# Half slabs, another order of the first tiles, turns in the second router, and token lists multiplied on TensorE, in a two-layer diffusion backbone

## The reference, cut to what matters

```python
mod = (silu_c @ ada_w[l] + ada_b[l])[:, None, :]
sh1, sc1, g1, sh2, sc2, g2 = jnp.split(mod, 6, axis=-1)
hx = modulate(rms_norm(x, norm_mix_w[l]), sh1, sc1)     # h * (1 + scale) + shift
mx = even_mixer(hx, hc, w_in[li], ...) if even else pool_mixer(hx, ...)
x = x + g1 * mx
x = x + g2 * moe_ffn(modulate(rms_norm(x, norm_ffn_w[l]), sh2, sc2), router_w, router_b, ...)

def moe_ffn(h, router_w, router_b, w_gate, w_up, w_down):
    combine = moe_route(flat, router_w, router_b)       # sigmoid scores, top 2 inside one group of 4
    for e in range(N_EXPERTS):
        hid = jax.nn.silu(flat @ w_gate[e]) * (flat @ w_up[e])
        out = out + combine[:, e:e + 1] * (hid @ w_down[e])
```

## Time and profile before

| | |
|---|---|
| median of 3 runs | 1142.43 us (1141.96 to 1145.59) |
| profiled execution | 1138.41 us, span 1136.4 us |
| TensorE busy, share of span | 1007.8 us, 89% |
| VectorE busy | 937.8 us, 83% |
| ScalarE busy | 627.1 us, 55% |
| GpSimd busy | 141.7 us, 12% |
| mean granted TensorE clock | 0.961 of full |

### The profile page before, as it was taken

How to read it: one execution, slowest core, us unless ns; L and a number is a source line. 1 busy time by engine, 2 the same in 40 slices (tenths; PEclk the granted TensorE clock), 3 DMA queues, 4 the chain that set the end, 5 groups by cost and what they waited for, 6 DMA issues and landing times. The chain is left out here.

```text
span 1136.4 us, 14202 instructions
## 1 busy us (share of the span) xinstructions
PE 1007.8 (89%) x4910; PEld 804.5 (71%) x4910; DVE 937.8 (83%) x1037; ACT 627.1 (55%) x770; POOL 141.7 (12%) x176
## 2 busy tenths in 40 slices
PE   5888999998898996899999999928799999999980
PEld 1467777786666774788888888827578888888870
DVE  4578997895697865799999999856689999999975
ACT  1535322323476234677777777533467777777841
POOL 0100210000010002510000000041440000000006
PEclk9899999998899998999999999969899999999995
DMA  9726878844200645899999999967399999999946
GB/s 370 270 75 222 282 253 289 289 167 153 89 1 1 224 192 184 278 401 413 413 415 414 414 413 414 347 241 287 114 331 411 415 413 414 414 414 414 413 200 241
DMA packets 148822, 332.46 MB, mean 293 GB/s; under 512 B 16956, under 2 KB 18948, under 8 KB 148648
## 3 DMA queue, kind: packets, MB, share of 16 engines
q1 hardware_dynamic: 125768, 277.99, 64.3%
q10 hardware_dynamic: 15520, 28.68, 7.1%
q0 software_dynamic: 7488, 25.19, 5.9%
HBM read 308.72 MB, written 23.15 MB: 292 GB/s over the span
## 5 line engine op out<-in xcount | busy, mean ns | idle before, releaser
L1984 DVE TENSOR_TENSOR w_lo<-ring,w_hi 128x2048 fp32r<-128x2048 f32 x192 | 432.8, 2287 | 25.5 <-ACT w_hi L1820 22.9
L1820 ACT CAST w_hi<-ring 128x2048 fp32r<-128x2048 f32 x192 | 364.4, 1914 | 144.9 <-DMA ring<-in_moe_w_up 52.3
L2095 PE MATMUL bank<-w_hi,xT_hi 128*128 128x512 f32 x512 | 203.4, 397 | 8.1 <-DVE xT_lo L1991 5.2
L2095 PE MATMUL bank<-w_hi,xT_lo 128*128 128x512 f32 x512 | 199.9, 390 | 0.0
L2095 PE MATMUL bank<-w_lo,xT_hi 128*128 128x512 f32 x512 | 199.4, 390 | 0.0
L1478 PE MATMUL bank<-ring_last_parts,arena_parts 128*128 128x512 f32 (+1 forms) x320 | 117.2, 397 | 5.6 <-DVE ring_parts L1070 3.1
L2095 PEld LDWEIGHTS bank<-w_hi,xT_hi 128*128 128x128 f32 x512 | 96.2, 188 | 29.8 <-DVE xT_lo L1991 6.9
L2095 PEld LDWEIGHTS bank<-w_hi,xT_lo 128*128 128x128 f32 x512 | 96.1, 188 | 20.9
L2095 PEld LDWEIGHTS bank<-w_lo,xT_hi 128*128 128x128 f32 x512 | 96.2, 188 | 19.0
L1478 PE MATMUL bank<-ring_parts,arena_parts 128*128 128x512 f32 (+1 forms) x256 | 100.3, 392 | 0.0
L1131 DVE SCALAR_TENSOR_TENSOR gate_b<-ring,silu_c,gate_b 128x512 f32<-128x512 f32 x126 | 95.5, 758 | 4.5
(11 more groups left out here) (270 smaller groups left out, 1505.7 us busy)
## 6 DMA issues: line engine op xcount, KB each, us to landing
ring<-in_moe_w_gate SPq DMA_DIRECT2D x64, 1024.0 KB
ring<-in_moe_w_down SPq DMA_DIRECT2D x64, 1024.0 KB, 11.8
ring<-in_moe_w_up SPq DMA_DIRECT2D x64, 1024.0 KB, 13.4
ring<-in_ada_w SPq DMA_DIRECT2D x19, 2048.0 KB, 9.4
y_scratch<-shared ACTq DMA_DIRECT2D x30, 512.0 KB, 6.8
ring<-in_w_in ACTq DMA_DIRECT2D x21, 512.0 KB, 4.4
shared<-in_ada_w SPq DMA_DIRECT2D x3, 2048.0 KB, 15.4
x_res<-in_x SPq DMA_DIRECT2D x8, 512.0 KB, 11.9
```

The lines of the kernel that those rows point to most:

```text
L1820: nc.scalar.copy(w_hi[:, buf(u, p), :], half(raw(e, p))).then_inc(s_hi, 3 if isinstance(e, int) and (e, p) == (-1, 3) else 1)
L1984: V.tensor_tensor(w_lo[:, buf(u, p), :], half(raw(e, p)), w_hi[:, buf(u, p), :].bitcast(F32), ALU.subtract).then_inc(s_lo, 3 if isinstance ...
L2095: last = pe.matmul(bank[:, b, :], xs[:, kk, :], ws[:, k, :], start=(kk == 0 and i == 0), stop=(kk == KD - 1 and i == 2))
```

## The change

Four parts. **Loads and sums:** the four slabs are loaded in halves, in the order `PRE_ORDER`, all of them ahead of the tokens; seven constant loads go from ScalarE's queue to SyncE's, behind x5, and the zeroing of the lists goes away. VectorE sums slab 3 and then the first half of slab 2; TensorE adds its own matmuls of slab 2's second half to the pick of that sum. **First tiles:** other orders on ScalarE, VectorE and TensorE; the spot (0, 3) stands just ahead of (1, 3), and from quarter 2 on ScalarE casts w_hi(n + 1) ahead of the load of quarter n + 2. **Router of layer 1:** square(3) ahead of copy_T(1), and transposes(t) ahead of logits(t − 1). **Lists:** the places of the two chosen experts of a token become half-precision one-hots `slot_of`; eight small matmuls with `listed` (token number where the expert is chosen) make all 16 lists in one bank. Expert 0 keeps its own direct list. The fetches take their rows from `lists` with no cast. The path for over 128 tokens is made anew on the same principle.

```diff
+        PRE_ORDER = ((3, 0), (0, 0), (3, 1), (0, 1), (1, 0), (1, 1), (2, 0), (2, 1))
+        spots.remove((0, NT - 1))
+        spots.insert(spots.index((1, NT - 1)), (0, NT - 1))
...
+                for j, hf in PRE_ORDER:
+                    k = slice(hf * KD // 2, (hf + 1) * KD // 2)
+                    sp.dma_start(pre_slab(j)[:, k], slab(ada_w[0], j * HALF)[:, k]).then_inc(m_pl[j][hf], 16)
                 load_rows_of(0)
                 load_rows_of(1)
-                sp.dma_start(pre_slab(2), slab(ada_w[0], 2 * HALF)).then_inc(m_pl[2], 16)
...
                     if t == 0:
+                        if 2 <= n + 1 < NQ:
+                            w_hi(n + 1)
                         if 3 <= n + 2 < NQ:
                             act.wait_ge(m_pu, used(n - 1))
                             load_w(act, n + 2)
-                        if 2 <= n + 1 < NQ:
-                            w_hi(n + 1)
...
                 rows_of_slab(0, 0)
+                dve.wait_ge(m_pre, 2)
+                sum_of_pre(2, 0, KD // 2)
+                rows_of_slab(1, 3)
+                rows_of_slab(2, 1)
                 xhat_of(0)
                 xhat_of(1)
-                rows_of_slab(1, 1)
-                w_lo(0)
-                rows_of_slab(2, 3)
                 rows_of_slab(3, 2)
+                xhat_of(2)
...
                 h_rest(0)
+                w_lo(0)
+                h_low(0)
                 h_rest(1)
-                xhat_of(2)
-                h_low(0)
                 xhat_of(3)
+                h_low(1)
                 h_rest(2)
-                h_low(1)
+                w_lo(1)
+                h_low(2)
                 h_rest(3)
-                h_low(2)
                 h_low(3)
-                w_lo(1)
...
+                rows_of_pre(0, 0).then_inc(m_pre, 1)
+                rows_of_pre(1, 0, KD // 2)
+                pick_pre(3, 1, True).then_inc(m_pre, 1)
+                rows_of_pre(1, KD // 2).then_inc(m_pre, 1)
+                rows_of_pre(2, KD // 2, stop=False)
+                pick_pre(2, 2, False).then_inc(m_pre, 1)
                 transpose_x(0)
...
                     fetch(0, idx[:])
                     nc.gpsimd.memset(mark[:], 0.0).then_inc(s_first_rows, 1)
+                    pool.wait_ge(s_lists, 1)
+                    for m in range(1, NE):
+                        u = m % 2
+                        if m >= 2:
                             pool.wait_ge(s_gt, m - 1)
                             pool.wait_ge(s_xg[u], 16 * (m // 2))
+                        fetch(u, lists[:, m:m + 1])
...
+                    for c in range(2):
+                        ins = V.tensor_tensor(slot_of[:, c], places.unsqueeze(1).to_broadcast([P, NT, P]),
+                                              cols(place[:, c, :], P), ALU.is_equal)
+                    ins.then_inc(s_slots, 1)
...
                     low(-1, 0, 0)
+                    dve.wait_ge(s_in_lists, 1)
+                    V.tensor_copy(lists[:], bank[:, LIST_BANK, 0:NE]).then_inc(s_lists, 1)
+                    low(-1, 0, 1)
+                    rows_low(0, 0, None)
+                    low(-1, 0, 2)
+                    low(-1, 0, 3)
                     rows_of_tokens()
-                    rows_low(0, 0, None)
-                    for p in range(1, 4):
-                        low(-1, 0, p)
                     weights_of_tokens()
...
-                    keep_busy(10)
+                    keep_busy(6)
                     rows_T(0, 16)
...
-                for t in range(NT):
+                for t in range(NT - 1):
                     act.wait_ge(p_xr, t + 1)
                     front1.square(act, t)
-                    if t >= 1:
-                        front1.copy_T(act, t - 1)
-                front1.copy_T(act, NT - 1)
+                front1.copy_T(act, 0)
+                act.wait_ge(p_xr, NT)
+                front1.square(act, NT - 1)
+                for t in range(1, NT):
+                    front1.copy_T(act, t)
```

More of the change, by code:

```diff
@@ L574, in build_program @@
             transposes_after.setdefault(projected(u) - 1 + 4, []).append(r)
-        m_ld = {n: sem(f"m_ld_{n}") for n in ("ident", "smallA", "smallB", "rope", "row", "gap", "zero")}
+        m_ld = {n: sem(f"m_ld_{n}") for n in ("ident", "smallA", "smallB", "rope", "row", "gap")}
         m_x = [sem(f"m_x{t}") for t in range(NK)]
@@ L824, in _ @@
                 h_first(0)
+                h_high(0)
                 h_first(1)
-                h_high(0)
+                h_high(1)
                 h_first(2)
-                h_high(1)
+                h_high(2)
+                w_hi(1)
                 h_first(3)
-                h_high(2)
                 h_high(3)
-                w_hi(1)
                 squares_of(4)
@@ new lines, in _ @@
+                    for c in range(2):
+                        ins = V.tensor_tensor(r_tmp[:, c], pick[:, c], pos, ALU.mult)
+                    link(ins)
+                    link(V.tensor_reduce(place[:], r_tmp[:], AX.X, ALU.add))
+                    dve.wait_ge(s_first, 1)
+                    V.tensor_copy(idx[:], bank[:, FIRST_BANK, 0:1]).then_inc(s_first_idx, 1)
+                    for c in range(2):
+                        ins = V.tensor_tensor(slot_of[:, c], places.unsqueeze(1).to_broadcast([P, NT, P]),
+                                              cols(place[:, c, :], P), ALU.is_equal)
@@ L1951, in rows_of_tokens @@
+                    ins.then_inc(s_slots, 1)
                     def rows_of_tokens():
-                        for c in range(2):
-                            ins = V.tensor_tensor(r_tmp[:, c], pick[:, c], pos, ALU.mult)
-                        link(ins)
-                        link(V.tensor_reduce(place[:], r_tmp[:], AX.X, ALU.add))
                         V.scalar_tensor_tensor(row_tmp[:, 0], e_sel[:], float(P), place[:], ALU.mult, ALU.add)
@@ L2257, in _ @@
                         pe.transpose(bank[:, 5, 0:P], ident[:], ident[:]).then_inc(v_d, 1)
+                        for b in range(MORE):
+                            pe.wait_ge(v_slot, 2 * b + 2)
+                            if b >= 1:
+                                pe.wait_ge(v_lists, b)
+                            for c in range(2):
+                                for t in range(NT):
+                                    last = pe.matmul(bank[:, LIST_BANK, 0:NE], slot_of[:, c, t, :], listed[:, c, t, :],
+                                                     start=(c == 0 and t == 0), stop=(c == 1 and t == NT - 1))
+                            last.then_inc(v_in, 1)
+                        pe.wait_ge(v_lists, MORE)
                         for e, b, n in blocks(pe):
```

211 lines of the change are left out of this document (98 added, 113 removed).

## The result

The changed kernel takes 1132.33 us, the median of 7 runs (1129.51 to 1136.84), against 1141.96 for the kernel before in the same comparison: a ratio of 0.9924, 95% interval 0.9898 to 0.9950. Timed twice more beside other kernels it gave 0.9941 (0.9920 to 0.9962) and 0.9939 (0.9913 to 0.9965). So it is faster by 0.6 to 0.8%, 6 to 9 us. I had forecast 1140.7, with a range from 1135.5. The direction was right and the size was wrong by about 5 to 7 us in differences (1.7 forecast, 6.3 to 8.6 measured).

The account below looks back on a forecast made before the run. The prediction took TensorE to bound the experts, so that only its waits elsewhere could pay; the front's +3.2, layer 1's router's −2.4 and the lists' −2.5 summed to −1.7 us, a median of 1140.7, range 1135.5 to 1145.0.

Parts of the forecast that it names:

- A: Front of layer 0: an early start lost again and a likely clock fall, +3.2 us, ends −5.5 and +11.
- the base: Front of layer 0: quarter 4's first matmul moves from 79.20 to 80.3, +1.0 us at full clock.
- the 2.2 us for the clock: Front, behind x4: about 4.5 us of TensorE work at clock 0.50 adds 2.2 us, quarter 4 at 82.5.
- the head start: Front: first projection matmul 5.5 us sooner, at 39.1; quarter 3's load then waits for spot (0,3) until 61.3.
- C: Layer 1's router: earlier square(3) and transposes start the sigmoid at 797.7 instead of 800.13, −2.4 us, between −1 and −3.
- M: Lists, both expert layers: without scatters the first experts' waits for weights go, −2.5 us, between −3.8 and +1.
- The gather of expert 1: Start of the experts: issued later, behind the lists' copy, +0.3 us per layer (0 to 0.9), 0.6 in all.
- the upper end of 0.9 per layer: Expert 1's fetch: VectorE shutting GpSimd out of the common port would cost 0.9 us per layer, making the lists' term −1.3.
- the filler's cut to six: Ahead of rows_T(0): keep_busy(10) to (6) costs 0.8 to 1.9 us per layer if the clock falls, otherwise nothing.
- rival (1): Front keeps full clock or part of its early start: +1.0 to −0.5 there, total −3.9 to −5.4, about 1138; chance 0.25.

Follow-up runs that it names:

- A and C: The changed kernel with the lists made by scatters again, as in the kernel before: 1136.15 us, ratio 0.9994 to before.
- C alone: The kernel before with only the two new orders in layer 1's router: 1134.66 us, ratio 0.9958.
- C and M: The kernel before with the new router orders and the lists multiplied on TensorE, front as before: 1130.86 us, ratio 0.9941 to before.
- A alone: The kernel before with only the new front (loads, sums, first tiles), zeroing of the lists kept on SyncE's queue: 1138.54 us, ratio 0.9999.
- A and M: The changed kernel with layer 1's router in its old order: 1134.60 us, ratio 0.9973 to before.
- scatters kept: The changed kernel with eight scatters per layer kept as idle work into a list nobody reads: 1135.23 us, ratio 0.9958 to before.
- the two edits: On the changed kernel, separately: spot (0,3) in its old place, 1127.63 us (again 1125.59); tile 4's work ahead of the quarter 0 buffer wait, 1127.43 us.
- before again: The kernel before, unchanged, timed and profiled again: 1138.75 us, ratio 1.0000.
- tile 4 early: The changed kernel with tile 4's work ahead of quarter 0's buffer wait (ScalarE) and w_lo(3) (VectorE), tile 5's second half too: 1127.43 us, ratio 0.9898 to before.

## Why the prediction was wrong

**A, the front (+3.2 forecast, 0 measured): two terms failed. The base, "Carried on, the first matmul of quarter 4 [...] falls on 80.3: +1.0 with the clock at full speed", was 2 us too late, and the 2.2 us for the clock were added whole, though waits behind it take over part of them.** In the first trace the steps up to there seem to hold: TensorE's start 8.98 (9.2 forecast), the first normalized tile 34.03 (35.1), the first projection matmul 38.08 (39.1), x4's transposes 55.47 (57.4) behind a pause of 3.63 (4.4), quarter 3's load at 60.97 (61.3), x5 at 67.27 (68.0) behind 3.55 (4.2). But the last two were forecast for full clock, and in this trace the clock fell in both places. The Trainium skill ("TensorE: Matmul & The Clock Gate", section "HAM oscillation — how this bites in real kernels") says the same of such waits, and the windows (0.57, and 0.50 from 68 to 72) agree; in the kernel's second trace, with a pause of 3.63 ahead of x5 too, they show 1.00.

That second trace is the test of the base. There the load is issued at 59.86, x5's transposes stand at 66.23 and quarter 4 at 78.24; with A and C, the other trace of this front without such a fall, quarter 4 stands at 78.40. That is −1.0 and −0.8 against 79.20, not +1.0, though in both the clock had been at 0.50 for a while from 47 on, ahead of x4. In the five traces of this front with falls quarter 4 begins 0.9 to 2.4 us later than 78.24 (79.16 to 80.65, never 82.5), and quarter 6 0.9 to 1.7 later. In the kernel before, TensorE waits 1.22 us for VectorE at 79.20 and 1.49 at 94.03, and VectorE's dense stretch begins at 71.72 in it and at 71.86 in the changed kernel, since it follows x5's transposes. TensorE's slow work after 67.27 ran beside that stretch and took over the first wait whole (there is none at 80.65) and 0.4 of the second. The row for 79.20 with its 1.22 was before me, and I read it as a position only. And the kernel before pays for falls too: in two of the five traces of the old front (C alone, and C and M) the clock stood at 0.50 for some 3.4 us around 55, and quarter 4 began at 80.39 and 80.47. Quarter 4 begins at 79.37 on average in the seven traces of the new front (the changed kernel's three, A alone, A and M, A and C, scatters kept), and at 79.48 in the five of the old one. That the first trace's load and x5 agreed with my positions was luck: they were forecast without a fall, and came that late only with one.

A smaller slip changed nothing: I wrote 2.4 us for a spot, and the trace has 1.39, which still hides a landing of 3.6 us behind six spots.

**What takes the head start was named rightly**, and the experiments show it twice: ScalarE's wait for quarter 0's buffer, ahead of quarter 3's load and tile 4's work. "From 82 on the projection is bound by TensorE, and what the front lost or gained goes through" held in the main: what the two edits gain at 84 is still seen at 288 (4.6 to 7.8 us ahead of before).

**C, the router (−2.4 forecast).** The traces give −2.3 in every kernel that has it, the sigmoid at 797.40 against 797.7 forecast. The times give 3.1 to 4.8, with intervals that hold 2.3 alone (up to 0.9981, 2.2 us). Right.

**M, the lists (−2.5 forecast).** The mechanism was right: the scatters held back the weights. The term was mis-sized, since I took both waits from one execution (1.63 and 1.26, where the second trace of the same kernel has 2.91 and 2.24). In the table, from 430 to 500 and from 800 to 850, the four other kernels with the scatters of before lie at +2.3, −0.2, +0.1, −0.4 and at +2.2, +1.1, +0.1, +0.1 (before again, A, C, A and C), the mean with the first profile's zeros +0.4 and +0.7; the twelve with lists on TensorE and no scatters lie on average at −1.6 and −0.5. The difference is 3.2 us, and the times say 3.4 alone and 4.6 in company. The gather of expert 1, which I had charged with 0.6, cost nothing in the first trace: it is issued at 445.53, and TensorE does not wait for it. It did in others: 0.58 us in the changed kernel's second trace, 1.31 with tile 4 early and 1.44 with the scatters kept, in layer 0 each time. The Trainium skill ("SBUF — State Buffer", section "SBUF: two separate sides") is what I had taken the upper end of 0.9 per layer from; the issue does take long (2.74 us, 2.95 before), and in the first trace nobody waits. What I named and left at zero, the filler's cut to six, shows at 446.16: the transposes took 1.97 at the low clock, and the changed kernel lost 1.6 us between 430 and 457 in that trace, 0.2 and 0.3 in its two other ones. Two more of the thirteen traces with six filler matmuls lose 0.9 there, and none of the four others with ten; no run keeps ten and changes nothing else, so that the cut did it isn't shown.

**The sum.** C and M as measured make 5.5 us in the traces (2.3 and 3.2) and 6.5 to 7.7 in the times (3.1, and 3.4 to 4.6), of the 6.3 to 8.6 of the whole; mine were 4.9. Charging 3.2 for A made the largest part of the miss. My rival (1), with the front at +1.0 or less, was the nearest.

## What to carry to other kernels

Before an added cost is summed, look at what waits behind it: where another engine ends the next waits, the cost runs beside them. Two positions that agree with a forecast don't confirm it when the trace holds an event that the forecast counted on top; look for an execution without the event. When a piece of work is moved later in a ring of buffers, look at who refills the buffer that it holds, and at what else stands behind that engine's wait: here moving one spot of six matmuls behind three others cost 4 to 6 us, nearly the whole head start. And a wait that depends on transfers needs a second profile before it becomes a term: this one was 1.63 and 2.91 us in two executions of the same kernel.

## What the runs showed of the hardware

I had not expected that equal executions differ by whole falls of the clock: the stretch at 296 to 300 ran at 0.55 in one profile of before and at 1.00 in the other, with a step of 2.8 us, and the profiles of one kernel end up to 2.6 us apart (spans of 1136.4 and 1139.0 us for before; 1131.2, 1129.2 and 1129.7 for the changed kernel). What decides whether a pause brings the clock down isn't settled by these runs; the pause of 3.35 us that stood ahead of 277.24 before did so in all 18 traces, but the fall began anywhere from 2.0 us before the pause's end to 1.0 after it. The pause ahead of x5 did so in the changed kernel's first trace (3.55 us) and not in its second (3.63). Beside eight scatters of four-byte entries, ScalarE's longest wait for a weights DMA at the first experts of a layer was 3.5 to 6.6 us in the five traces with the lists of before, and at most 2.8 us in the twelve without scatters; whether it is the scatters' packets or GpSimd's work on them wasn't told apart.

How long GpSimd takes to issue an indirect DMA goes by what VectorE does at that moment. In the changed kernel the issue at 445.53, begun during a `w_lo` (445.18 to 447.46), took 2.74 us and ended 0.81 after it; that at 458.12, begun in the middle of one, 1.89; that at 472.11, begun just ahead of one, 0.94. Over the 18 traces 158 of the 162 issues that begin during a `w_lo` end some 0.8 us behind it.
